# Two more gate projections ahead of the merge, one of them in front of the mixer's levels, in a two-layer hybrid decoder

## The reference

```
h = x @ w_in                       # split into the inputs of the four branches
a = pool_mixer(p_in, ...)          # trailing means, per-group linear
b = hgrn2_mixer(hq, hf, hi, hg)    # gated linear recurrence, in chunks
c = gmlp_mixer(gu, gv, ...)        # spatial gating
d = fox_mixer(fq, fk, fv, ff)      # forgetting attention, 4 heads x 4 query blocks
br = stack([a, b, c, d])
gates = sigmoid(x @ w_gate + b_gate)             # 4 branches x 1024 channels
merged = einsum('bsmw,mwd,bsmd->bsd', br, w_branch, gates)
mix = merged @ w_out
x = layer_norm(ALPHA * x + mix, ...)             # then peer_ffn and layer_norm
```

## Time and profile before

| | us |
|---|---|
| runs | 3932.8, 3936.03, 3936.2 (median 3936.03) |
| profiled execution | 3931.17 |
| its span | 3929.4 |
| mixer and merge of layer 0 | about 251 to 640 of the span |
| mixer and merge of layer 1 | about 2204 to 2595 of the span |
| TensorE busy | 3823.6 (97%) |
| VectorE busy | 2744.8 (70%) |
| mean granted TensorE clock | 0.99 |

### The profile page before, as it was taken

How to read it: one execution, slowest core, us unless ns; L and a number is a source line. 1 busy time by engine, 2 the same in 40 slices (tenths; PEclk the granted TensorE clock), 3 DMA queues, 4 the chain that set the end, 5 groups by cost and what they waited for, 6 DMA issues and landing times. The chain is left out here.

```text
span 3929.4 us, 53536 instructions
## 1 busy us (share of the span) xinstructions
PE 3823.6 (97%) x19618; PEld 3344.9 (85%) x19618; DVE 2744.8 (70%) x5316; ACT 1478.7 (38%) x2124; POOL 1348.2 (34%) x1064
## 2 busy tenths in 40 slices
PE   8999999999999999999999999999998999999999
PEld 7877787899899999988878677888998999999887
DVE  3257545299979888878642555352999898888887
ACT  2243432244663333333322434222437633333332
POOL 1012000066765555543000210000657565555440
PEclk9999999999999999999999999999999999999999
DMA  4211322254579999999732214232545799999995
GB/s 149 92 57 57 133 93 106 106 192 158 188 255 374 362 363 338 344 350 354 252 129 91 75 41 137 94 127 90 187 177 181 260 373 364 357 345 345 349 353 213
DMA packets 319797, 846.02 MB, mean 215 GB/s; under 512 B 20608, under 2 KB 118912, under 8 KB 294528
## 3 DMA queue, kind: packets, MB, share of 16 engines
q1 hardware_dynamic: 245888, 575.26, 41.5%
q0 software_dynamic: 73728, 268.47, 18.2%
HBM read 755.05 MB, written 88.60 MB: 215 GB/s over the span
## 5 line engine op out<-in xcount | busy, mean ns | idle before, releaser
L89 PE MATMUL bank<-xT_low,u_high 128*128 128x384 f32 (+1 forms) x2144 | 733.0, 342 | 8.0 <-DVEq L1906 4.7
L90 PE MATMUL bank<-xT_high,u_high 128*128 128x384 f32 (+1 forms) x2144 | 727.9, 340 | 0.0
L91 PE MATMUL bank<-xT_high,u_low 128*128 128x384 f32 (+1 forms) x2144 | 727.7, 339 | 0.0
L89 PE MATMUL bank<-v_low,w_high 128*128 128x512 f32 x1536 | 597.8, 389 | 0.9 <-DVE v_low L1933 0.9
L91 PE MATMUL bank<-v_high,w_low 128*128 128x512 f32 x1536 | 598.1, 389 | 0.0
L90 PE MATMUL bank<-v_high,w_high 128*128 128x512 f32 x1536 | 598.1, 389 | 0.0
L1140 POOL TENSOR_TENSOR u_low<-merged,u_high 128x1024 fp32r<-128x1024 f32 x96 | 244.1, 2557 | 906.6 <-ACT u_high L1135 906.4
L1206 POOL DMA_INDIRECT far_rows<-peer_v_dram,far_index x256 | 386.9, 1511 | 417.3 <-DVE x_far L1230 371.9
L1206 POOL DMA_INDIRECT far_rows<-peer_u_rows_dram,far_index x256 | 360.7, 1409 | 329.0 <-DVE far_dots L1212 281.2
L1933 DVE TENSOR_TENSOR v_low<-v_raw,v_high 128x1024 fp32r<-128x1024 f32 x256 | 301.6, 1221 | 187.4 <-ACT v_high L1844 187.4
L1844 ACT ACTIVATE v_high<-v_raw 128x1024 fp32r<-128x1024 f32 x256 | 257.3, 1053 | 449.4 <-PE bank L91 444.3
(11 more groups left out here) (400 smaller groups left out, 7000.4 us busy)
## 6 DMA issues: line engine op xcount, KB each, us to landing
merged<-peer_u_dram SPq DMA_DIRECT2D x128, 1024.0 KB, 7.8
v_raw<-peer_v_dram SPq DMA_DIRECT2D x128, 1024.0 KB
gates_scratch<-stage SPq DMA_DIRECT2D x24, 2048.0 KB, 9.6
G<-gates_scratch SPq DMA_DIRECT2D x64, 768.0 KB
mg_raw<-w_merge_dram SPq DMA_DIRECT2D x32, 768.0 KB, 4.3
hidden_scratch<-ahead_hid SPq DMA_DIRECT2D x60, 384.0 KB, 2.4
hid<-hidden_scratch SPq DMA_DIRECT2D x30, 768.0 KB, 7.9
first_raw<-w_in_dram SPq DMA_DIRECT2D x20, 1024.0 KB, 5.9
```

What stands on the lines that cost most here:

```text
L89: nc.tensor.matmul(out, lh, rl, start=first, stop=False)
L90: nc.tensor.matmul(out, lh, rh, start=False, stop=False)
L91: return nc.tensor.matmul(out, ll, rh, start=False, stop=last)
```

## The change

Two constants go up: nine gates stand in front of the levels (before: eight), and sixteen are computed in the mixer (before: fourteen). So the merge has no gate projection left in branches 0 and 1. The table `gates_at` is written anew: what gate 8 was in the levels gate 9 is now, and so on; the part "keys" has a whole projection in place of half of one, and so has "end". On TensorE the wait for the pooling weights is behind gate 0. ScalarE copies out gate 13 ahead of the tiles, and gates 14 and 15 around the normalization. In the merge, branch 2 is written out (before: a loop of four rounds); the split of branch 2 stays behind unit 14. The core of the diff:

```diff
-GATES_EARLY = 8
-GATES_AHEAD = 14
+GATES_EARLY = 9
+GATES_AHEAD = 16
@@ merge_stage
-            if m < 2:
+            if m < 3:
                 for n in range(KT):
                     body(KT * m + n, n, n % 2)
                 return
@@ SyncE
-                assert GATES_AHEAD + 2 == 2 * KT
+                assert GATES_AHEAD == 2 * KT
...
-                    with sp.Fori(1 if m == 2 else 0, KT // 2) as i:
+                    with sp.Fori(2 if m == 2 else 0, KT // 2) as i:
@@ ScalarE and VectorE
-                        if isinstance(n, int) and n == GATES_AHEAD:
+                        if isinstance(n, int) and n == 2 * KT - 2:
                             split_branch(2)
@@ mixer_stage, TensorE
-                pe.wait_ge(params_in["poolw"], 16)
                 for g in range(WT):
                     if g % 2 == 0:
                         multiply_gate(pe, g // 2)
+                    if g == 0:
+                        pe.wait_ge(params_in["poolw"], 16)
                     pe.wait_ge(diff_ready, g + 1)
...
                 multiply_gate(pe, 7)
-                gates_at = {("level", 0): [(8, 0, 5)], ("level", 1): [(8, 5, 8)], ("level", 2): [(9, 0, 3)],
-                            ("level", 3): [(9, 3, 8), (10, 0, 8)], ("level", 4): [(11, 0, 8)],
-                            ("keys", 0): [(12, 0, 4)], ("tile", 1): [(12, 4, 8)],
-                            ("norm", 0): [(13, 0, 4)], ("end", 0): [(13, 4, 8)]}
+                multiply_gate(pe, 8)
+                gates_at = {("level", 0): [(9, 0, 5)], ("level", 1): [(9, 5, 8)], ("level", 2): [(10, 0, 3)],
+                            ("level", 3): [(10, 3, 8), (11, 0, 8)], ("level", 4): [(12, 0, 8)],
+                            ("keys", 0): [(13, 0, 8)], ("tile", 1): [(14, 0, 4)],
+                            ("norm", 0): [(14, 4, 8)], ("end", 0): [(15, 0, 8)]}
@@ mixer_stage, ScalarE
                 fox_steps(fox, ("keys", 0))
+                keep_gate(act, 13)
                 for t in range(NT):
                     act.wait_ge(o_mm, t + 1)
                     A(tmp[0][:, t, :], bank[t % 2][:], ACT.Copy).then_inc(o_kept, 1)
                     fox_steps(fox, ("tile", t))
-                    if t == 1:
-                        keep_gate(act, 12)
                 act.wait_ge(ss_ready, 1)
                 A(rms[:], ss[:], ACT.Sqrt).then_inc(ss_sqrt, 1)
                 fox_steps(fox, ("norm", 0))
+                keep_gate(act, 14)
                 act.wait_ge(params_in["normg"], 16)
-                keep_gate(act, 13)
+                keep_gate(act, 15)
```

More of the change, by code:

```diff
@@ L2366, in _ @@
                     if i == 2:
-                        keep_gate(act, 8)
+                        keep_gate(act, 9)
                 act.wait_ge(lvl_d, NL + 1)
@@ L2370, in _ @@
                 A(flat(tmp[0]), flat(tmp[0]), ACT.Exp).then_inc(lvl_e, 1)
-                keep_gate(act, 9)
+                keep_gate(act, 10)
                 fox_steps(fox, ("level", NL - 1))
-                keep_gate(act, 10)
+                keep_gate(act, 11)
                 act.wait_ge(kd_d, 1)
@@ L2378, in _ @@
                 fox_steps(fox, ("level", NL))
-                keep_gate(act, 11)
+                keep_gate(act, 12)
                 for t in range(NT):
```

## The result

The changed kernel takes 3940.19 us (median of 16 runs, 3937.0 to 3949.07), the kernel before, on the same chip, 3932.3 (16 runs, 3926.21 to 3936.2). The ratio is 1.0025, with a 95% interval from 1.0018 to 1.0031 (7 to 12 us): slower, by 7.9 us between the medians. The prediction was 3942 us: +6.2 us on a median of 3936.0 in the first three runs of the kernel before, against +7.9 on 3932.3 now. The profiled execution of the changed kernel took 3946.2 us with a span of 3944.5; it lies in the upper part of its runs' spread, so its stages add up to more than the medians differ by.

The account below looks back on a forecast made before the run. TensorE, busy 97% of the span, was taken as the bound. Mixer +9.8 and merge -6.7 gave +3.1 us per layer, +6.2 in all on a median of 3936.0: 3942 us, eight in ten between 3930 and 3953.

Parts of the forecast that it names:

- Merge, two gates and the new wait: Merge: two gates leave, -11.3 us; TensorE waits for branch 2's split before unit 16, +2.9 us, per layer.
- The clock behind that wait: Merge, behind the wait before unit 16: TensorE's clock falls to 1.2 GHz, +1.7 us per layer (0 to 2.0).
- The mixer's front: Gates 0 to 7: gate 0 starts 3.2 us earlier, but only 0.3 us is gained at gate 7's end.
- Level 0: First level of the mixer: gate 8 now lies in front, so the level is done 2.3 us later.
- GpSimd's low parts: GpSimd's low parts of gate weights hold VectorE: +0.3 us at level 0, +1.3 at the first tile, +0.5 of clock.
- Keys and end: Mixer: half a projection more in "keys", +2.8 us; gate 15 at the end waits for its bank, +2.6 us.
- The mixer's sum: Mixer, per layer: 2.3 + 0.3 + 1.3 + 0.5 + 2.8 + 2.6 = +9.8 us.
- The total: Both layers: mixer +9.8 and merge -6.7 give +3.1 us per layer, +6.2 in all.
- The idle time: Rival, chance 0.10: idle time in the mixer and before level 0 takes the added gates; -5.0 us per layer, 3926 us.
- The front's gain: Rival, chance 0.20: the front's 3.2 us arrive whole at gate 7; +0.2 us per layer, 3936 us.
- The slow side's mechanism: Rival, chance 0.22: GpSimd holds VectorE for whole 2.4 us at level 0 and tile 0, clock falls; +18.4 us, 3954 us.

Follow-up runs that it names:

- e8: Changed kernel with branch 2 split in quarters behind units 9 to 12 and gate 13 copied out behind the first tile; 3927.74 us, ratio 0.9990.
- e10: e8 with three eighths of gate 13 ahead of the last level's wait, and gate 12 copied out before that level's steps; 3920.28 us, ratio 0.9972.
- e1: Changed kernel with the split of branch 2 cut in quarters behind units 9 to 12; 3928.1 us, ratio 0.9987 to the kernel before.
- e2: Changed kernel with the whole split of branch 2 behind unit 12 rather than 14; 3930.58 us, ratio 0.9994 to the kernel before.
- e3: Changed kernel with the wait for the pooling weights ahead of gate 0 again; 3938.64 us, ratio 1.0018 to the kernel before.
- e4: Changed kernel with gate 13 copied out and gate 15's weights rounded behind the first tile; 3934.73 us, ratio 1.0008 to the kernel before.
- e7: Changed kernel with eight gates in front rather than nine, and two whole gates at the mixer's end; 3955.23 us in five runs, ratio 1.0058.
- e5: Kernel before with only the wait for the pooling weights moved behind gate 0; 3933.28 us, ratio 1.0003.
- e6: Kernel before, still fourteen gates in the mixer, but nine of them in front of the levels; 3934.76 us, ratio 1.0007.
- e11: e8 with eight gates in front rather than nine, and two whole gates at the mixer's end; 3935.6 us, ratio 1.0009 to the kernel before.

## Why the prediction was right, point by point

- **Merge, two gates and the new wait.** Predicted at full clock -11.3 + 2.9 = -8.4 per layer. Measured in the table above: 192.15 to 183.65 (means of two layers), -8.5; without the wait (e8, e10) the merge is 11.3 us shorter, as summed. The wait was 2.99 us and, in layer 1, 3.08. It is shown by e1, which takes it away, and by e2, which turns it into one of 1.0 and 1.3 us.
- **The clock behind that wait.** Predicted +1.7. Measured 3.6 and 1.7 in the changed kernel; in the other three kernels that keep the wait (e3, e4, e7) 3.7 and 1.7, 1.7 and 1.7, 0 and 3.8. The mean of the eight is 2.2, so the prediction was a little too small, and the spread is larger than its range of 0 to 2.0. The merge gave 5.3 and 6.2 us and not 6.7.
- **The mixer's front.** Predicted 0.3 us of the 3.2. One trace can't tell so little: against what it was before plus a gate of 5.65, TensorE was ready for level 0 some 0.7 us sooner behind the mixer's start in layer 0, and 0.5 us later in layer 1. Over all traces it was ready at 62.4 us with the wait for the weights ahead of eight gates and at 62.3 with the wait behind gate 0; with nine gates at 67.6 and 67.8. So nothing came, within some 0.7 us of scatter: the second pooling product waited for VectorE as the prediction said (3.22 us; 1.73 in layer 1), and the gating for another 1.5 to 2.2 us. e3 and e5 show it from both sides. The half clock behind the first gate didn't vanish, it moved behind the second pooling product and became shorter: 0.72 from 262 to 268 in layer 0.
- **Level 0.** Predicted start 319.25, measured 319.34, at the short duration. Counted from the mixer's start that is 67.7 predicted, 67.3 and 68.2 measured. e6, e7 and e11 show that a gate in front costs about what the sum had: e7 and e11 pay 3.2 and 3.6 per layer for taking it away and putting it at the end, 3.3 was the sum.
- **GpSimd's low parts.** At level 0 predicted +0.3, measured 0.65: L2432 took 1.87 us rather than 1.22, and TensorE's wait at L2181 grew from 0.6 to 1.27. At the first tile predicted +1.3, measured 1.26, and e4 shows the mechanism by moving GpSimd's work. The page "GPSIMD Engine Reference" of the Trainium skill, section "1. Specifications", limits the contention to VectorE instructions with two SBUF inputs or in a two-port mode; L2414 has one SBUF input and was held, so by that page it must be of the second kind. The 1.3 us of its wait rightly stayed in the sum. The 0.5 us of clock behind it did not come: in none of the eight mixers of the changed kernel, e1, e2 and e3 did the clock fall there.
- **Keys and end.** Predicted 2.8 + 2.6 = 5.4. The bank's wait was 0.50 us as predicted. The transposes began 10.9 us later against the mixer's start, and 11.4 in layer 1, where about 9.8 was predicted. One small thing was missed: the first branch product waited 2.95 us (layer 1: 2.57) and not 2.47. In layer 0 ScalarE entered the merge 0.81 us after its last work, 0.43 before. That is +0.5 and +0.1.
- **The mixer's sum.** Predicted +9.8. At full clock it grew by 12.1 us (185.4 to 197.5, over six mixers of before and eight of the changed kernel and e1 to e3). The prediction's own terms give +11.0 at full clock, since its +2.3 at level 0 nets 1.7 us of slow clock that go. What was short by about 1 us is, as far as the rows show, the low part at level 0 (0.35), the entry of the merge (0.3) and the front's 0.3. Against it the clock gave back 3.0 us per mixer over the same traces, where the prediction had +0.5 at the tile and -1.7 at level 0. (The -1.7 came: none of the eight had half clock in level 0.) So the work was 1.1 us too small and the clock 1.8 us too dear, and the two errors cancel: +9.1 measured. That part of the agreement is luck.
- **The total.** 9.1 - 8.5 + 2.2 = +2.8 us per layer by these means, 3.1 predicted; twice that is 5.6 us, and the medians say 7.9. The profiled execution alone would say +5.6 per layer, since in this pair the clock gave back only 0.9 us per mixer and took 2.7 per merge. Split by TensorE's busy and idle time, over the same traces: its work at full clock is 11.3 us longer in the mixer and 11.2 shorter in the merge, as it must be; its idle time grew by 0.5 and 3.1 us; low clock under its matmuls took 2.7 us less in the mixer and 1.9 more in the merge. So the change costs the idle time that it makes, above all the 3 us before unit 16. The clock over all runs says so too: 0.9904 in the changed kernel, 0.9901 in 35 runs of the kernel before beside e1 to e4, so about 38 and 39 us lost of an execution. The clock's share in one layer is known to some 2 us only, in the prediction and behind it.
- **The time and the odds.** 3942 us is 1.8 us too high, although the change came out 1.7 us larger than forecast, because the first three runs of the kernel before stood 3.7 us above the later sixteen; that is luck too. The largest chance, 0.56, was given to no measurable change, and slower had 0.34. Slower is what came: the interval of 7 to 12 us leaves out zero, and 7.9 us is just what the prediction took as the least that can be told.
- **One reading.** The 5.3 us of the earlier trace rows are of 250 to 450 us. One of their four waits, 0.5 us at 339, lies ahead of the window from 343 to 440, so 4.8 us of that window's 6.6 are the attention step's. Nothing in the sum hangs on it.
- **The rivals.** The idle time did not take the gates by itself; e10 shows that it takes them if the order puts them in front of the wait. The front's gain was not kept (e5). The slow side's mechanism, a whole 2.4 us lost each time, did not happen: only the part of GpSimd's instruction that was left when VectorE's began was lost, 0.65 and 1.26 us. "TensorE: Matmul & The Clock Gate", section "What's actually happening", in the Trainium skill, puts the ramp at under 1% of a typical kernel's span and advises against fitting it. For the size of the kernel the traces agree (mean clock 0.990 to 0.993, so 0.7 to 1.0% of the span lost). For a change of 0.25%, 7.9 us, the 3 to 14 us in each mixer are as large as the change.

## What to carry to other kernels

Work that leaves a saturated stretch costs the same where it goes, and uncovers what lay beside it: ask at each head of a stage which side job was hidden by the work that goes, and cut that job into pieces that fit the units left. Work pays in idle time only if it stands in program order ahead of the very wait that idles, and if its own inputs and bank are free by then; nine matmuls of 2.1 us, moved some 14 us forward into such a place, made the mixer 1.3 us shorter. Removing the first wait of a chain gives nothing when the next link waits for another engine: look for the next row of that engine before you book the gain.

## What the runs showed of the hardware

- Some VectorE instructions on SBUF wait for a GpSimd instruction that runs, and then for all that is left of it. A copy of 128x8 elements that began at 264.19 took 2.33 us, beside a GpSimd instruction from 264.09 to 266.49; alone it takes 0.16. In all thirteen traces every such case of L2414's TENSOR_SCALAR (128x384), of this copy and of L2432's TENSOR_TENSOR was held (10, 13 and 26 cases in which GpSimd had longer to run than VectorE needed). Neither size nor SBUF alone decides: the RECIPROCAL of 128x1 just ahead of L2414, SBUF to SBUF, took its usual 0.15 us in the middle of GpSimd's 415.29 to 417.64, and so did all 18 of its kind. VectorE's COPY_PREDICATED out of PSUM took its usual 0.73 us at 323.11, in the middle of GpSimd's 322.17 to 324.53 (all from the timeline of the changed kernel).

```profile
264.19 2.33 DVE L2440 COPY tmp<-tmp 128x8 f32<-128x8 f32 x1
...
264.09 2.40 POOL L2095 TENSOR_TENSOR gl_wl<-gl_raw,gl_wh 128x1024 fp32r<-128x1024 f32 x1 [2.10 <-ACT gl_wh L2091]
...
323.11 0.73 DVE L2518 COPY_PREDICATED att<-lvl_mask,bank 128x512 f32<-128x512 uint32 x1 [0.16 <-PE bank L2266]
...
416.08 0.15 DVE L2413 RECIPROCAL fsum<-fsum 128x1 f32<-128x1 f32 x1
```

- The same waits of TensorE were followed by the full clock in one kernel and by half of it in another (e8 and e10 at the last level), and a wait of 2.55 us in e8 by none. The loss of a stage is mostly near 1.7, 3.4, 5.1, 6.8, 8.5 or 12.0 us, and where the clock falls differs between the two layers of one execution. What decides it is open.
